# A decoder step on one core: the half tile of the mixing stage goes first, in plain single precision and two column groups

## The reference, cut to what matters

```
a = y @ w_out                                  # (512) @ (512, 2048)
out = a[..., :1024] * sigmoid(a[..., 1024:])
x = x + out
# then hier_moe(rmsnorm(x)): router logits (20 columns) -> best group, best two of its four experts,
# SwiGLU experts of width 256, weighted sum, residual add, final RMSNorm
```

## Time and profile before

| | us |
|---|---|
| median of 3 runs | 867.94 (866.84 to 869.41) |
| the profiled execution | 860.02 |
| its span, first to last instruction | 858.3 |
| mixing stage in it, on TensorE | from 201 to 425 |
| TensorE busy (matmul) | 790.9 |

### The profile page before, as it was taken

One profiled execution on the slowest core, in us unless ns is written; L12 is line 12 of the kernel. 1 busy time (PEld: TensorE's weight loads), 2 busy tenths in 40 slices (PEclk: granted clock), 3 DMA queues, 4 the chain that ended last, 5 costly groups with the idle time before them and its releaser, 6 DMA issues. The chain is left out here.

```text
span 858.3 us, 15035 instructions
## 1 busy us (share of the span) xinstructions
PE 790.9 (92%) x4238; PEld 625.6 (73%) x4238; DVE 597.6 (70%) x1126; ACT 414.2 (48%) x773; POOL 330.4 (38%) x409
## 2 busy tenths in 40 slices
PE   5899998998999999999818999999999999999982
PEld 3678875655877878887516888888888888888861
DVE  6997768998433436555675688787866878876852
ACT  6546743115425535334304467466564566655630
POOL 2920001002000000330633477766766767666532
PEclk9999999999999999999957999999999999999995
DMA  7754514888724324333127657766767768875721
GB/s 239 223 172 147 161 25 98 263 176 190 310 90 148 125 96 148 111 112 136 51 66 289 240 206 267 266 218 215 281 195 258 263 224 292 292 261 193 285 93 76
DMA packets 57782, 160.99 MB, mean 188 GB/s; under 512 B 22480, under 2 KB 26960, under 8 KB 51024
## 3 DMA queue, kind: packets, MB, share of 16 engines
q1 hardware_dynamic: 34704, 112.75, 40.6%
q0 software_dynamic: 22976, 47.05, 15.6%
HBM read 128.80 MB, written 62.40 MB: 223 GB/s over the span
## 5 line engine op out<-in xcount | busy, mean ns | idle before, releaser
L1237 PE MATMUL pbig<-WH,xgH 128*128 x320 | 131.1, 410 | 1.4 <-ACT xgH L889 1.4
L1238 PE MATMUL pbig<-WL,xgH 128*128 x320 | 126.8, 396 | 0.0
L1137 PE MATMUL pbig<-w2H,ysH 128*128 128x512 f32 (+1 forms) x272 | 111.6, 410 | 2.9 <-DVE ysL L1568 1.6
L515 POOL DMA_INDIRECT records<-rec,at_rec x34 | 34.5, 1016 | 205.2 <-DVEq L1711 196.0
L1138 PE MATMUL pbig<-w2L,ysH 128*128 128x512 f32 (+1 forms) x272 | 107.1, 394 | 0.0
L1139 PE MATMUL pbig<-w2H,ysL 128*128 128x512 f32 (+1 forms) x272 | 106.7, 392 | 0.0
L573 POOL DMA_INDIRECT x_sums<-xg,recs x36 | 77.1, 2141 | 37.4 <-DVE xg L1828 29.1
L1718 DVE SCALAR_TENSOR_TENSOR WL<-WR,gf_p,WH 128x512 f32 (+1 forms) x128 | 86.3, 745 | 3.3 <-POOL recs L542 1.8
L853 ACT ACTIVATE WH<-WR,gf_p 128x512 f32 (+1 forms) x128 | 80.5, 712 | 2.9 <-DMA WR<-in_w_gu 1.4
L1241 PE MATMUL pbig<-WH,xgL 128*128 x320 | 81.3, 396 | 0.0
L1608 DVE TENSOR_TENSOR x<-pbig,sg 128x1024 f32<-128x1024 f32 (+1 forms) x17 | 20.8, 1225 | 80.1 <-PE pbig L1139 79.0
(11 more groups left out here) (292 smaller groups left out, 1691.7 us busy)
## 6 DMA issues: line engine op xcount, KB each, us to landing
WR<-in_w_gu SPq DMA_DIRECT2D x32, 1024.0 KB, 6.8
WR<-in_w_dn SPq DMA_DIRECT2D x16, 1024.0 KB, 5.9
xT<-in_x_cols SPq DMA_DIRECT2D x16, 512.0 KB, 4.6
low<-in_x_rows SPq DMA_DIRECT2D x16, 512.0 KB, 3.8
U<-in_x_rows SPq DMA_DIRECT2D x16, 512.0 KB, 5.1
x_mid<-x SPq DMA_DIRECT2D x16, 512.0 KB, 2.7
x_sums<-x SPq DMA_DIRECT2D x16, 512.0 KB, 3.9
w<-in_w_out SPq DMA_DIRECT2D x1, 4096.0 KB, 12.5
```

The costliest lines, as they stand in the source:

```text
L1137: pe.matmul(pbig[0:rows, n, :], ysH[b][:, k, 0:rows], w2H[n][:, k, :], start=(k == 0), stop=False)
L1237: pe.matmul(pbig[:, 6, :], xgH[b][:, k, :], WH[:, w], start=(k == 0), stop=False)
L1238: pe.matmul(pbig[:, 6, :], xgH[b][:, k, :], WL[:, w], start=False, stop=False)
```

## The change

The tile of 64 rows becomes tile 0 and the 16 whole tiles follow as 1 to 16. Tile 0 is projected by `c_half`: plain fp32 matmuls straight from y and the unsplit `w2`, the two column blocks of a pair (gate columns 1024 to 1535 and 1536 to 2047, then value columns 0 to 511 and 512 to 1023) going to partitions 0 to 63 and 64 to 127 of one PSUM bank. So x of tile 0 lies as 128 partitions of 512 columns, row r in partitions r and r + 64. Its gate, its square and its transposes are of half size; the two halves' sums of squares are added by a matmul with `pair` (`c_half_sum`), and VectorE's `c_mix(0)` waits for that. `f` = `s` - 1 counts the whole tiles. Only the y of the first whole tile is split ahead of the loops. Token numbers of the routing columns (`tokf`, `tokB`), the rows filed and the memset of the unused half move with the new order. SyncE waits for `c_half` before it loads expert weights over the place of `w2`.

```diff
+        pair = sb("pair", [P, P])
...
+            half_rows = [(slice(h * ST, (h + 1) * ST), slice(h * 512, (h + 1) * 512)) for h in range(2)]
+
+            def c_load(s):
+                b = s % 2
+                if s >= 2:
+                    sp.wait_ge(S["x2_done"], s - 1)
+                if s == 0:
+                    for p, c in half_rows:
+                        sp.dma_start(xr[0][p, 0:512], x_rows[TF * P:NT, c]).then_inc(S["xr_in0"], 16)
+                else:
+                    sp.dma_start(xr[b], x_rows[(s - 1) * P:s * P, :]).then_inc(S[f"xr_in{b}"], 16)
...
+                    if s == 0:
+                        for p, c in half_rows:
+                            sp.dma_start(xD[TF * P:NT, c], x2[0][p, 0:512]).then_inc(S["x2_st0"], 16)
+                    else:
+                        sp.dma_start(xD[(s - 1) * P:s * P, :], x2[b][:, :]).then_inc(S[f"x2_st{b}"], 16)
...
             sp.wait_ge(S["w2_lo"], CB)
             sp.wait_ge(S["w2_hi"], CB)
+            sp.wait_ge(S["a_done"], 2)
             for c in range(CUTS):
                 src = w_gu[0][:, c * CW:(c + 1) * CW] if c < UP_CUTS else w_dn[0]
                 sp.dma_start(WR[:, c * CW:(c + 1) * CW], src).then_inc(S[f"wts{c}"], 16)
...
+            for tok, base in ((tokf, 0), (tokB, int(BIG))):
+                pool.iota(tok[:, 0:1], [[0, 1]], base=base + TF * P, channel_multiplier=1, allow_small_or_imprecise_dtypes=True).then_inc(S["consts"], 1)
+                pool.iota(tok[:, 1:TT], [[P, TF]], base=base, channel_multiplier=1, allow_small_or_imprecise_dtypes=True).then_inc(S["consts"], 1)
...
+            def c_gate(s):
+
+                if s == 0:
+                    act.wait_ge(S["a_done"], 1)
+                    act.activation(sg[:, 0:512], pbig[:, 4, :], ACT.Sigmoid).then_inc(S["sig_done"], 1)
+                    return
+                act.wait_ge(S["x2_done"], s)
+                act.wait_ge(S["ssq_done"], s)
...
+            def c_routed(s):
+                rows = P if s else LAST
+                act.wait_ge(S["rl_done"], s + 1)
+                act.wait_ge(S["dchc"], NC * s + NC)
+                act.activation(logit[0:rows, s, :], pbig[0:rows, 6, 256:276], ACT.Copy,
+                               scale=rr[0:rows, s:s + 1]).then_inc(S["rl_evac"], 1)
...
             c_y_hi(0, 1)
-            for part in range(2):
-                c_y_hi(1, part)
-            for t in range(TT):
-                c_gate(t)
-                if t >= 1:
-                    c_turned(t - 1)
-                    c_parts(t - 1)
-                if t - 1 in ROUTE_A:
-                    exps(ROUTE_A.index(t - 1))
-                if t >= 1:
-                    c_routed(t - 1)
-                c_square(t)
-                if t + 2 < TT:
+            for s in range(TT):
+                c_gate(s)
+                if s >= 1:
+                    c_turned(s - 1)
+                    c_parts(s - 1)
+                if s - 1 in ROUTE_A:
+                    exps(ROUTE_A.index(s - 1))
+                if s >= 1:
+                    c_routed(s - 1)
+                c_square(s)
+                if s + 1 < TF:
                     for part in range(2):
-                        c_y_hi(t + 2, part)
-                if 4 <= t < 4 + CUTS:
-                    act.wait_ge(S[f"wts{t - 4}"], 16)
-                    cut_hi(EW, t - 4)
+                        c_y_hi(s + 1, part)
+                if 4 <= s < 4 + CUTS:
+                    act.wait_ge(S[f"wts{s - 4}"], 16)
+                    cut_hi(EW, s - 4)
             c_turned(TF)
             c_parts(TF)
...
+            def c_half(ks):
+
+                if ks[0] == 0:
+                    pe.wait_ge(S["wout_in"], 16)
+                    pe.wait_ge(S["y_in"], 16 * (CB - 1) * 8)
+                    pe.wait_ge(S["gelu_done"], G - 2)
+                for bank, n in ((4, 2), (5, 0)):
+                    for k in ks:
+                        if k == CB - 1:
+                            pe.wait_ge(S["y_tail"], 16 * 8)
+                        y = yflat[:, k, TF * P:NT] if k < CB - 1 else ylast[:, TF * P:NT]
+                        for h in range(2):
+                            mm = pe.matmul(pbig[h * ST:(h + 1) * ST, bank, :], y, w2[:, k, (n + h) * 512:(n + h + 1) * 512],
+                                           start=(k == 0), stop=(k == CB - 1))
+                    if k == CB - 1:
+                        mm.then_inc(S["a_done"], 1)
+
+            def c_proj(s, ns, ks=range(CB)):
+                f = s - 1
+                b = f % 2
                 for n in ns:
-                    if n == 2 or t == 0:
...
+                            pe.wait_ge(S["ys_lo"], 2 * f + 2)
+                        pe.matmul(pbig[:, n, :], ysH[b][:, k, :], w2H[n][:, k, :], start=(k == 0), stop=False)
+                        pe.matmul(pbig[:, n, :], ysH[b][:, k, :], w2L[n][:, k, :], start=False, stop=False)
+                        mm = pe.matmul(pbig[:, n, :], ysL[b][:, k, :], w2H[n][:, k, :], start=False, stop=(k == CB - 1))
                     if k == CB - 1:
                         mm.then_inc(S["a_done"], 1)
...
+            def c_turn(s):
+                b = s % 2
+                pe.wait_ge(S["x2_done"], s + 1)
+                if s == 0:
+                    pe.wait_ge(S["gelu_done"], G)
+                    for k in range(4):
+                        mm = pe.transpose(pbig[:, 7, k * P:(k + 1) * P], x2[0][:, k * P:(k + 1) * P], ident[:, :])
+                    mm.then_inc(S["xt_done"], 2)
+                    return
...
+
+                pe.wait_ge(S["fold_set"], 2)
+                pe.wait_ge(S["ssq_done"], 1)
+                pe.matmul(pbig[:, 5, 0:1], pair[:, :], ssq[:, 0:1], start=True, stop=True).then_inc(S["half_ss"], 1)
+
...
-            for t in range(TT):
-                if t == 0:
-                    c_proj(0, (2, 3, 0, 1), range(CB - 1))
-                    c_proj(0, (2, 3, 0, 1), (CB - 1,))
-                    pe.wait_ge(S["gelu_done"], G)
-                    continue
-                c_proj(t, (2, 3))
-                if t >= 1:
-                    c_turn(t - 1)
-                c_proj(t, (0,))
-                if t == 1:
+            blocks = (2, 3, 0, 1)
+            c_half(range(CB - 1))
+            c_proj(1, blocks, range(CB - 1))
+            c_half((CB - 1,))
+            c_proj(1, blocks, (CB - 1,))
+            c_turn(0)
+            c_half_sum()
+            for s in range(2, TT):
+                c_proj(s, (2,))
+                if s == 2:
                     pe.wait_ge(S["wr_scaled"], KD)
-                if t >= 1:
-                    c_logit(t - 1)
-                if t == TF:
+                    c_logit(0)
+                c_proj(s, (3,))
+                if s == 2:
+                    c_fold(0)
+                c_turn(s - 1)
+                c_proj(s, (0,))
+                c_logit(s - 1)
+                if s == TF:
                     positions(2)
-                c_proj(t, (1,))
-                if t >= 1:
-                    c_fold(t - 1)
-                if t in POS_AT:
-                    positions(POS_AT.index(t))
+                c_proj(s, (1,))
+                c_fold(s - 1)
+                if s in POS_AT:
+                    positions(POS_AT.index(s))
             c_turn(TF)
             c_logit(TF)
             c_fold(TF)
...
@@ -1588,30 +1635,39 @@
             for k in range(KD):
                 ts(wr_sb[:, k, :], wr_sb[:, k, :], gf_p[:, k:k + 1], None, ALU.mult).then_inc(S["wr_scaled"], 1)
             dve.tensor_reduce(fold[:, :], ident[:, :].rearrange("p (n c) -> p c n", c=32), AX, ALU.add).then_inc(S["fold_set"], 1)
+            halves = [ident[:, h * ST:(h + 1) * ST].unsqueeze(1).to_broadcast([P, 2, ST]) for h in range(2)]
+            tt(pair[:, :].rearrange("p (r c) -> p r c", r=2), halves[0], halves[1], ALU.add).then_inc(S["fold_set"], 1)
             dve.memset(rr[:, :], 0.0).then_inc(S["rr_zero"], 1)
             dve.wait_ge(S["rr_zero"], 1)
...
                 dve.nop().then_inc(S["x2_done"], 1)
                 dve.wait_ge(S["ssq_done"], t + 1)
+                if t == 0:
+                    dve.wait_ge(S["half_ss"], 1)
+                total = ssq[:, t:t + 1] if t else pbig[:, 5, 0:1]
                 mean, y_, h_, t2 = nv[0:rows, 0:1], nv[0:rows, 1:2], nv[0:rows, 2:3], nv[0:rows, 3:4]
-                lk(ts(mean, ssq[0:rows, t:t + 1], 1.0 / D, EPS, ALU.mult, ALU.add))
+                lk(ts(mean, total, 1.0 / D, EPS, ALU.mult, ALU.add))
...
-                if hi == TT:
-                    dch(dve.memset(EX[LAST:P, :, TF, :], 0.0))
+                if lo == 0:
+                    dch(dve.memset(EX[LAST:P, :, 0, :], 0.0))
...
             c_y_lo(0, 1)
-            for part in range(2):
-                c_y_lo(1, part)
             for t in range(TT):
                 if t == TF:
                     route_b(2)
                 c_mix(t)
-                if t + 2 < TT:
+                if t + 1 < TF:
                     for part in range(2):
```

(50 more changed lines are left out.)

127 lines of the change are left out of this document (54 added, 73 removed).

## The result

| | before | after |
|---|---|---|
| median of the timed runs | 867.92 (865.54 to 870.81, 12 runs) | 863.44 (861.42 to 867.26, 12 runs) |
| the profiled execution | 860.02 | 861.47 |
| its span | 858.3 | 859.6 |

The ratio is 0.9946 (0.9932 to 0.996): by the medians 4.5 us faster, outside the predicted 864.6 to 870.6. So there are two things to explain: a gain of some 2.3 us where 0.4 was forecast, and some 2 us more in the first timing alone. The profiled executions do not show the gain, because the changed kernel's contains late instructions that the other's does not; we come to them.

A forecast was written before the change was run, and what follows sets the result against it. TensorE, busy 92% of the span, was taken as the bound, with only the mixing stage's two ends able to move. Head -3.4, clock +1.6 and tail +1.4 gave -0.4 us, so 867.5; range 864.6 to 870.6.

The forecast's parts named there:

- head without the clock: Start of the mixing stage: half tile fills both old waits, c_proj(3) begins at 238.6 against 241.98; gains 3.4 us.
- the new wait: TensorE before the third tile: split of its y stands behind VectorE's c_mix(0), which awaits the half sum; 3.1 us.
- tail: End of the mixing stage: last tile now whole, so transposes, logits and evacuations take longer; +1.4 us, +0.4 at full clock.
- Part 3, the clock: Behind TensorE's 3.1 us wait before the third tile, granted clock most likely falls to half; +1.6 us, bounds 0 and 3.2.
- the rival that it stays at full: Clock stays full after TensorE's wait before the third tile; -3.0 to -2.0 us, 864.9 to 865.9; chance 0.12.
- the doubled clock: Rival: half clock behind TensorE's wait before the third tile lasts twice as long; another +1.6 us, 869.1; chance 0.20.
- A pair: Two fp32 matmuls in c_half, one on each half of the output partitions, run side by side in 0.96 us, at most 1.01.
- The second wait: TensorE before c_proj(3): c_logit(1) waits some 0.7 us for ScalarE's chain of squares, splits, gates and evacuation.
- the pairs do not run side by side: Rival, in c_half: sixteen matmuls at 0.96 in place of eight pairs; +7.7 us, 875.2; chance 0.05.
- the rival by which 32 loads stand bare: In c_half: weight loads do not overlap matmuls on the same rows; 0.14 us each, 4.4 in all, 871.9; chance 0.03.
- The late chain on ScalarE: Rival: squares, splits and gates stay late, 0.7 us again per tile; four tiles cost 2.8 us, 870.3; chance 0.10.
- The shorter wait: Rival: VectorE or ScalarE makes the second split before the half sum, so neither 3.1 nor 1.6 is paid; 862.8; chance 0.08.

The follow-up runs named there:

- one column group: Changed kernel with both matmuls of each half-tile pair sent to output partitions 0 to 63; x of the half tile wrong; 884.7 us total, the place itself 10.44 us.
- the early split: Changed kernel with the y of the second whole tile split ahead of the loops again; 855.38 us, ratio 0.9947; on another occasion 852.54 us, 0.993.
- its version with a whole tail: Kernel before, with the last tile's transposes, logits, fold and their evacuations done for 128 rows in place of 64; ratio 1.0004.

## Why the prediction was wrong

**What each term came to.** Forecast, and the rows of all profiles of the unaltered changed kernel:

| | forecast | measured |
|---|---|---|
| head without the clock | -3.4 | -4.4 (46.3 to 41.9, three executions) |
| clock behind the new wait | +1.6 | 0 in three executions, +1.56 in one |
| middle | 0 | +0.1 |
| tail | +1.4 | +1.6 (25.57, mean of six profiles of changed kernels without lateness, experiments among them, less 23.97) |
| sum | -0.4 | -2.7, or -1.1 where the clock falls |

**The first step that failed is Part 3, the clock.** The price is right, 1.56 us for 1.6 in the one profile of the changed kernel where it came. What was wrong is that it was charged to the likeliest case, with 0.12 for the rival that it stays at full. Of the seven profiles with the wait of 2.82 us (the three experiments with another order or column group in them), it stayed in five and fell in two. The prediction read the length of a wait as what decides, from two rows of a fall, behind 3.20 and 1.91 us, and one of none, behind 1.56 and 1.21. It does not decide between 1.6 and 3.1 us. Behind 1.58 us the clock fell in one profile of the changed kernel and behind 1.59, at the same instruction, it stayed in another; and the changed kernel's first profile has, in the experts' stage, full clock behind 3.10:

```profile
382.02 0.45 PE L1221 MATMUL pbig<-EE,upper 128*128 128x80 f32 x2 [1.59 <-DVEq L1724]
...
839.68 0.50 PE L1309 MATMUL pbig<-WH,hTH 128*128 x1 [3.10 <-DVE hTL L1863]
...
839.70:845.20 5.50, 3.03 (x12) 2.19 (x12) 3.53 (x3) 1.33 (x4) 1.80 (x3) 1.00 0.26 98
```

Behind the 3.20 us in the state-space stage and behind 7.59 it was at half every time. What tells the executions apart stays open here.

**The second is in the sum: "7.9 above that execution, and I take the difference over to it".** The changed kernel's timed runs are 2.0 us above its profile, not 7.9, since that profile has 6.2 us of lateness in it and the profile of before has none. Head, clock and tail as measured, -2.7 us, taken off 867.94, give 865.2, which is inside the range; what carried the first timing out of it is a further 2.1 us that none of the terms holds (below). Inside the prediction one more sum is off: the bounds of the terms with the clock charged once give 865.9 to 868.5, not 866.3 to 869.1 (the upper of these has the doubled clock in it).

**The head was mis-sized by 1.0 us,** in three terms, all on the dear side. A pair is 0.88 us, not 0.96, and so below the lower bound given for it (a fourfold one-pass matmul of 0.24 us): 0.4 in the eight pairs, by the measured 5.30 and 1.87 us for 5.7 and 1.9. The new wait is 2.82 for 3.1. The second wait is 0.17 for 0.7, as the chain on ScalarE ended 10.5 us after the third tile's start (222.27 to 231.69 + 1.06) where the prediction had 10.8, while TensorE came to it 0.3 later than forecast. Small stretches between took the rest back. The forecast's order of events holds in each step: both waits filled, the new one behind the half sum, the second one behind the evacuation, then the old rhythm.

**The tail** was right: the logits 2.65 us after the turn for the forecast 2.6 (426.89 to 429.54), and +1.6 in all for 1.4.

**The rivals.** That the pairs do not run side by side fell: one column group costs 10.44 us, two 5.30. With it falls the rival by which 32 loads stand bare: the whole half tile takes 7.2 us with its loads in it. The late chain on ScalarE fell: the wait is 0.16 to 0.17 once, and the middle is 0.1 us longer. The shorter wait fell; the early split shows that its whole length is on the path. The rival that the clock stays full is what three of four profiles of the changed kernel show; it gave 864.9 to 865.9, and the gains of 2.4, 1.7 and 2.3 us, taken off the 867.94 of the prediction, make 865.5, 866.2 and 865.6.

**The other 2 us of the first timing** are in none of the terms. The numbers that bear on them: the kernel before had 867.9 and 868.6 us on two occasions and 859.0 to 859.1 on three; the changed one 863.4 and 866.6, and 856.4 and 856.9. So against its own time without lateness (859.05 and 856.65), and if nothing else differed between the occasions, the kernel before paid 8.9 and 9.6 us, the changed one 6.8 and 9.9. By the changed kernel's own traces of the two occasions the lateness is 6.2 and 10.4 us. The measured 4.5 is then 2.4 and a difference of 2.1 in lateness. (Clock at half behind a late instruction counts as lateness here.) For the changed kernel traces and timings agree within 0.6 us, but the share of the kernel before is argued from its timings, since none of its traces shows lateness, not even the first one, beside which its timed runs are 7.9 us longer; the nearest, its version with a whole tail, shows 7.7 us where its timing has about 9 (869.49 less 859.05 and 1.4). Why the lateness differs between two occasions stays open, and so does what makes the instructions late: ScalarE's row names no instruction or transfer of the program. The experiments moved nothing of it on purpose.

## What to carry to other kernels

When the last thing that a stage needs is prepared on other engines, give the bottleneck a piece of work that needs no preparation, even in a dearer number format: most of the gain here is the order. (The same cheap arithmetic with the half tile left last was not tried.) But look at what the moved piece now stands ahead of on the helpers; the split of the next operand slid behind a reduction that waits for TensorE, and moving it in front gives another 3 us in the traces, so the early split is the version to keep. And before a small change is judged, time the kernel before and after on more than one occasion, and profile both on each: one timing here was twice the change's size.

## What the runs showed of the hardware

- Plain fp32 matmuls of 64 columns against 512 take 0.87 us alone; two in different column groups take 0.88 us together. A later one in the free group starts ahead of an earlier one queued for the busy group, here by 0.9 us.
- Behind the same wait of 2.82 us on the same instruction, the granted clock was full in five executions and half for 3.4 us in two, at a cost of 1.56 and 1.49 us. Elsewhere it fell behind 1.58 us and stayed full behind 3.10.
- On some occasions single instructions of ScalarE in the mixing stage start some 2 to 4 us late with no releaser in the program, at the same tiles and by the same sum in three kernels on one occasion (middle 189.2 us for 180.8), and cost 6 to 10 of this kernel's 860 us.
